# A hybrid attention and SSM layer on one core: a fourth slot in the norm stage, gate products over units 1 to 21, two slots from unit 23, and three smaller edits

## The reference

```python
mod = jax.nn.silu(c) @ w_ada + b_ada            # c: 9 vectors of 2048, w_ada 2048 x 6144
shift, scale, gate = jnp.split(mod, 3, axis=-1)
h = _rmsnorm(x, g_pre) * (1 + scale[:, None]) + shift[:, None]
proj = h @ w_in                                 # q, k, v, z_a, z_b, xbc, dt, r_a, r_b
# A: dilated window attention of three groups (window 128, 512, 2048; dilation 1, 4, 16), 8 heads, times silu(z_a), @ w_o_a
# B: convolution, SSD scan, then
y = y + xs * d_skip[:, None]
yg = y * silu(z_b), in 8 groups of 256 columns
yg = yg * lax.rsqrt(jnp.mean(yg * yg, axis=-1, keepdims=True) + NORM_EPS)
p_b = (yg * g_ssm) @ w_o_b
merged = jax.nn.sigmoid(r_a) * p_a + jax.nn.sigmoid(r_b) * p_b
y_out = x + gate[:, None] * _rmsnorm(merged @ w_o, g_post)
```

## Time and profile before

| | before |
|---|---|
| runs | 3129.91, 3122.58, 3134.31 us |
| profiled execution | 3134.02 us, its span 3132.2 us |
| mean granted PE clock | 0.981 |
| busy: PE, DVE, POOL, ACT | 96%, 65%, 35%, 27% |
| start of unit 1 | 138.91 us |
| start of units 22 and 23 | 454.48 and 467.30 us, 12.8 us for a plain unit |
| a unit with a gate product that waits for nothing | 14.55 us (units 2 to 3: 155.23 to 169.77) |

### The profile page before, as it was taken

The page is one execution under the profiler, slowest core; times in us unless marked ns, Lnnn a source line. Parts: engine busy times, 40 slices in busy tenths (PEclk is TensorE's granted clock), DMA queues, the critical chain, the costliest instruction groups (busy, mean ns, idle before and its releaser), DMA issues. The chain is left out here.

```text
span 3132.2 us, 52927 instructions
## 1 busy us (share of the span) xinstructions
PE 3016.7 (96%) x23068; PEld 2848.9 (91%) x23068; DVE 2036.4 (65%) x2027; ACT 847.8 (27%) x1026; POOL 1099.2 (35%) x368
## 2 busy tenths in 40 slices
PE   5899999999999999999999999999999999999996
PEld 4798999899999999999999999999999989999785
DVE  3301799998994988988888766887777854212202
ACT  2111222232323223233222133333333332212221
POOL 0133233333322333333343343444444423333332
PEclk8899999999999999999999999999999999999998
DMA  8768786654445786646667566666556655766643
GB/s 316 282 245 312 293 300 243 221 201 140 150 134 192 259 292 235 208 180 236 252 238 248 187 228 218 223 217 231 197 196 229 222 193 198 280 248 235 240 170 113
DMA packets 222396, 704.89 MB, mean 225 GB/s; under 512 B 28675, under 2 KB 131835, under 8 KB 172731
## 3 DMA queue, kind: packets, MB, share of 16 engines
q1 hardware_dynamic: 159622, 471.33, 43.9%
q0 software_dynamic: 5248, 174.60, 14.0%
q10 hardware_dynamic: 57296, 55.59, 5.3%
HBM read 630.85 MB, written 245.17 MB: 280 GB/s over the span
## 5 line engine op out<-in xcount | busy, mean ns | idle before, releaser
L1310 PE MATMUL acc<-act,w_hi 128*128 128x288 f32 x5808 | 1742.5, 300 | 18.0 <-POOL w_lo L866 17.9
L1311 PE MATMUL acc<-act,w_hi 128*128 128x288 f32 x5808 | 1715.1, 295 | 0.0
L1312 PE MATMUL acc<-act,w_lo 128*128 128x288 f32 x5808 | 1715.0, 295 | 0.0
L866 POOL TENSOR_TENSOR w_lo<-w_raw,w_hi 128x2048 fp32r<-128x2048 f32 (+1 forms) x209 | 958.0, 4584 | 1986.7 <-ACT w_hi L918 1986.5
L1310 PEld LDWEIGHTS acc<-act,w_hi 128*128 128x128 f32 x5808 | 1092.5, 188 | 43.6 <-issue 20.7
L1311 PEld LDWEIGHTS acc<-act,w_hi 128*128 128x128 f32 x5808 | 1092.7, 188 | 1.8
L1312 PEld LDWEIGHTS acc<-act,w_lo 128*128 128x128 f32 x5808 | 1091.6, 188 | 0.7
L918 ACT ACTIVATE w_hi<-w_raw 128x2048 fp32r<-128x2048 f32 (+1 forms) x209 | 384.7, 1841 | 512.4 <-PE acc L1312 194.4
L1722 DVE TENSOR_TENSOR side<-side 128x2048 f32<-128x2048 f32 x96 | 323.7, 3372 | 70.9 <-DMA side<-in_vals_t 57.8
L1693 DVE TENSOR_TENSOR side<-side 128x2048 f32<-128x2048 f32 x96 | 334.3, 3482 | 51.1 <-DMA side<-in_keys_t 47.2
L984 ACT ACTIVATE ev<-acc 128x576 f32<-128x576 f32 x144 | 93.7, 651 | 787.9 <-PE acc L1312 776.4
(11 more groups left out here) (291 smaller groups left out, 2683.1 us busy)
## 6 DMA issues: line engine op xcount, KB each, us to landing
w_raw<-in_w_in_t SPq DMA_DIRECT2D x160, 1024.0 KB, 7.7
out_s_kv<-in_cache_a_w POOLq DMA_DIRECT2D x80, 1632.0 KB, 9.0
side<-in_keys_t SPq DMA_DIRECT2D x52, 1024.0 KB, 7.3
side<-in_vals_t SPq DMA_DIRECT2D x52, 1024.0 KB, 7.4
w_raw<-in_w_ada_t SPq DMA_DIRECT2D x48, 1024.0 KB, 7.6
out_s_kv<-in_cache_a_w POOLq DMA_DIRECT2D x24, 1344.0 KB, 8.6
w_raw<-in_w_o_b_t SPq DMA_DIRECT2D x16, 1024.0 KB, 7.2
w_raw<-in_w_o_t SPq DMA_DIRECT2D x16, 1024.0 KB, 9.0
```

Of the source, the lines that this page charges most:

```text
L866: nc.gpsimd.tensor_tensor(wl[:, u % 2, 0:kt, 0:cols], raw[:, SLOT[s], 0:kt, 0:cols], wh[:, u % 2, 0:kt, 0:cols].bitcast(F32), ALU.subtract ...
L1310: nc.tensor.matmul(out, wh[:, c, k, 0:cols], high, start=(k == 0), stop=False)
L1311: nc.tensor.matmul(out, wh[:, c, k, 0:cols], low, start=False, stop=False)
L1312: mm = nc.tensor.matmul(out, wl[:, c, k, 0:cols], high, start=False, stop=(k == kt - 1))
```

## The change

The table of slots now has four slots in the norm stage; the fourth lies in a part of `side` that is free there. Gate products are given to the units of `GATE_UNITS`: 1, 2, 3, 5, 6, 7, 9, 10, 12, 13, 14, 16, 17, 18, 20, 21. The units from 23 (`GATES_END + 1`) to `A0 + 3` share two slots, where this began at 111 before. `seen` keeps SP closer to the unit that runs from unit 23 on (6 half units where it was 8), and the store of the gate moves to half unit 48 from 38. `d_skip` comes from an array of 128 x 16 laid out by the host, in one load. In the SSM groups DVE adds the two squares and PE multiplies the sum with the ones. The rectangles of `BAND` are replaced by whole products.

```diff
+GATE_UNITS = [1 + n * 22 // NGATE for n in range(NGATE)]
+GATES_END = GATE_UNITS[-1] + 1
...
-    if 1 <= _u <= NGATE:
-        STREAM.append(("g", _u - 1))
+    if _u in GATE_UNITS:
+        STREAM.append(("g", GATE_UNITS.index(_u)))
...
+PSLOTS = 4
...
-    _few = _kind == "u" and BLOCK0 <= _n < A0 + 4
-    if _few:
-        _slot = _next[1] % 2
-        _next[1] += 1
+    _few = _kind == "u" and GATES_END + 1 <= _n < A0 + 4
+    if _s <= NADA:
+        _slot = _s % PSLOTS
+    elif _few:
+        _slot = (_n + A0) % 2
     else:
+        if _kind == "u" and _n == A0 + 4:
+            _next[0] = 2
         _slot = _next[0] % 3
...
-BAND = ((0, 0, 64), (2, 64, 128), (1, 32, 64), (1, 64, 96), (3, 96, 128))
...
+        fourth = side[:, 15744:15744 + D].rearrange("p (k n) -> p k n", n=P)
+
+        def slot(s):
+
+            return fourth if SLOT[s] == 3 else raw[:, SLOT[s], :, :]
...
-                if s >= 3:
+                if s >= PSLOTS:
                     slot_free(s)
...
+                        else:
+                            sp.wait_ge(gate_out, 16)
...
-                    with nc.allow_non_contiguous_dma(reason="one value a descriptor, once"):
-                        for hh in range(2):
-                            sp.dma_start(dsk[64 * hh:64 * hh + 64, :], A["d_skip"][0:1, hh:SH:2].to_broadcast((64, KT))).then_inc(const_in, 16)
+                    sp.dma_start(dsk, A["d_skip_t"]).then_inc(const_in, 16)
...
-                lag = 8 if u < BLOCK0 else 6 if u < A0 + 2 else 2 if u < A0 + 4 else 4
-                return max(0, 2 * min(u, NGATE + 2) - 4, 2 * u - lag)
+                lag = 8 if u < GATES_END + 1 else 6 if u < A0 + 2 else 2 if u < A0 + 4 else 4
+                return max(0, 2 * min(u, GATES_END + 1) - 4, 2 * u - lag)
...
-                    if half == 2 * NGATE + 6:
+                    if half == 2 * GATES_END + 4:
...
-                    if n == 0:
-                        nc.tensor.matmul(ps_s[:, 0:512], qk[:, 0, r:SEQ:4], qk[:, 3, :], start=True, stop=True)
-                    else:
-                        for x, i0, i1 in BAND:
-                            nc.tensor.matmul(ps_s[i0:i1, x * P:(x + 1) * P], qk[:, 0, 4 * i0 + r:4 * i1:4], qk[:, 3, x * P:(x + 1) * P],
-                                             start=True, stop=True)
+                    nc.tensor.matmul(ps_s[:, 0:512], qk[:, 0, r:SEQ:4], qk[:, 3, :], start=True, stop=True)
...
-                    for x, i0, i1 in BAND:
-                        nc.tensor.matmul(ps_w[i0:i1, P:2 * P], pT[:, x, i0:i1], vP[:, x, :], start=False, stop=False)
+                    for x in range(4):
+                        nc.tensor.matmul(ps_w[:, P:2 * P], pT[:, x, :], vP[:, x, :], start=False, stop=False)
...
-                    pe.wait_ge(ysq_d, g + 1)
+                    pe.wait_ge(ysum, g + 1)
...
-                        for j in range(2):
-                            mm = nc.tensor.matmul(bank[:, 0:HALF], ones[:, :], ysq[:, j, half * HALF:(half + 1) * HALF],
-                                                  start=(j == 0), stop=(j == 1))
+                        mm = nc.tensor.matmul(bank[:, 0:HALF], ones[:, :], ysq[:, 0, half * HALF:(half + 1) * HALF], start=True, stop=True)
...
+                if o == 18:
+                    dve.wait_ge(ysq_d, g + 1)
+                    TT(ysq[:, 0, :], ysq[:, 0, :], ysq[:, 1, :], ALU.add).then_inc(ysum, 1)
```

More of the change, by code:

```diff
@@ L416, in phase_all @@
         c_in, v_in, x_in, const_in = sems("c_in", "v_in", "x_in", "const_in")
-        w_in, ra_in = sems("w_in0", "w_in1", "w_in2"), sems("ra_in0", "ra_in1", "ra_in2")
+        w_in, ra_in = sems("w_in0", "w_in1", "w_in2", "w_in3"), sems("ra_in0", "ra_in1", "ra_in2")
         c_act, c_t, v_t, set_up, pool_set = sems("c_act", "c_t", "v_t", "set_up", "pool_set")
@@ L442, in phase_all @@
         st_t, st_c, p_out = sems("st_t", "st_c", "p_out")
-        yz, ysq_d, ss_t, rt, yr, yn, y_out = sems("yz", "ysq_d", "ss_t", "rt", "yr", "yn", "y_out")
+        yz, ysq_d, ysum, ss_t, rt, yr, yn, y_out = sems("yz", "ysq_d", "ysum", "ss_t", "rt", "yr", "yn", "y_out")
         ma_d, mr_in, mr_d = m.sem("ma_d"), sems("mr_in0", "mr_in1"), m.sem("mr_d")
@@ L518, in _ @@
                     weights(0)
-                if s >= 3:
+                if s >= PSLOTS:
                     slot_free(s)
-                sp.dma_start(raw[:, SLOT[s], :, :].rearrange("p k n -> p (k n)"), A["w_ada_t"][(n % 2) * KT + n // 2]).then_inc(w_in[SLOT[s]], 16)
+                sp.dma_start(slot(s).rearrange("p k n -> p (k n)"), A["w_ada_t"][(n % 2) * KT + n // 2]).then_inc(w_in[SLOT[s]], 16)
             sp.dma_start(causal[:, :], A["causal"]).then_inc(const_in, 16)
@@ L782, in _ @@
                     weights(u)
-                if 1 <= u <= NGATE:
-                    gate_weights(u - 1)
+                if u in GATE_UNITS:
+                    gate_weights(GATE_UNITS.index(u))
                 if u == 1:
@@ L843, in ssm @@
                     if g == 0:
-                        pool.wait_ge(const_in, 176)
+                        pool.wait_ge(const_in, 160)
                     nc.gpsimd.tensor_tensor(Bm, Bt[0:SAMP, 0, :].unsqueeze(1).broadcast_to((SAMP, NB, P)),
@@ L1208, in partial_sums @@
                     q = 32 * (k % 4)
-                    mm = nc.tensor.matmul(ps_s[q:q + 32, (n % 2) * 512:(n % 2) * 512 + P], c32[:, k, :], raw[:, SLOT[src], k, :],
+                    mm = nc.tensor.matmul(ps_s[q:q + 32, (n % 2) * 512:(n % 2) * 512 + P], c32[:, k, :], slot(src)[:, k, :],
                                           start=(k < 4), stop=(k >= KT - 4))
@@ L1571, in _ @@
                 attention(2 * u)
-                if 2 <= u <= NGATE + 1:
-                    gate_rows(u - 2)
+                if u - 1 in GATE_UNITS:
+                    gate_rows(GATE_UNITS.index(u - 1))
                 for g, o in ssm_steps(2 * u):
@@ L1582, in _ @@
                     ssm(g, o)
-                if 1 <= u <= NGATE:
-                    gate(u - 1)
+                if u in GATE_UNITS:
+                    gate(GATE_UNITS.index(u))
                 if u == FOLD0 // 2:
@@ L1854, in dt_part @@
                 if half == 2 * BLOCK0 + 5:
-                    dve.wait_ge(const_in, 176)
+                    dve.wait_ge(const_in, 160)
                     dve.wait_ge(evac, EVACS[u])
@@ L2088, in _ @@
                         low_oa(k)
-                if half % 2 and 1 <= u <= NGATE:
-                    gate_partials(u - 1)
-                if half % 2 == 0 and 2 <= u <= NGATE + 1:
-                    gate(u - 2)
+                if half % 2 and u in GATE_UNITS:
+                    gate_partials(GATE_UNITS.index(u))
+                if half % 2 == 0 and u - 1 in GATE_UNITS:
+                    gate(GATE_UNITS.index(u - 1))
                 for n in grains.get(half - KEYS0, ()):
@@ L2153 @@
          "c_prompt", "c_sample", "b_ada", "g_pre", "g_post", "conv_w", "conv_b", "dt_bias", "a_log",
-         "d_skip", "g_ssm")
+         "g_ssm")
 OUTS = (("y_prompt", (1, SEQ, D)), ("y_sample", (NB, NT, D)),
@@ L2194, in layouts @@
     out["keys_t"], out["vals_t"] = keys, vals
+    out["d_skip_t"] = np.ascontiguousarray(np.repeat(inputs["d_skip"][0].reshape(KT, 2).T, P // 2, axis=0))
     for name in ("w_o_a", "w_o_b"):
```

## The result

The changed kernel took 3100.36 us in the median (3099.99 to 3103.39), the kernel before, run in turn with it, 3130.52: a ratio of 0.9907, interval 0.9892 to 0.9922. That is 30 us, inside the range I gave (3093 to 3128) and on the side I forecast, but the sum of my terms had 18. The profiled execution's span went from 3132.2 to 3098.9 us. The page has PE at 2994.1 us (before 3016.7): 22.6 us less of work and of work at the lower clock together, and some 11 us less waiting.

A forecast was written before the change was run, and what follows sets the result against it. It took TensorE (PE) as the bound, busy 3016.7 of 3132.2 us, so only less PE work or waiting pays. The terms summed to -17.9 us, from the median 3129.9 to 3112 us, range 3093 to 3128.

The forecast's parts named there:

- Norm stage: Before unit 1: a fourth slot shortens waits for w_ada tiles, -10 us; unit 1's weights load later, +0.5.
- rival 1: Norm stage: the DMA queue was full already, so 3 us gained instead of 10; 3119 us, chance 0.17.
- Gate stage: Gate products in units 1 to 21: fewer stalls for POOL, but late DVE copies cancel them; 0 us (-10 to +10).
- Rival 2: Gate stage turns bad: late DVE copies hold PE in units 19 to 22, half clock follows; +10, 3122 us, chance 0.13.
- Two slots: From unit 23: weight loads wait for a later unit, but slack hides it; 0 us.
- d_skip: Near 1790 us: one load in place of two removes PE's wait for POOL and the lost clock; -7.1 us.
- rival 5: The d_skip load was not the cause; small loads around the weight load slow it; 3119 us, chance 0.06.
- SSM groups: Half the ones products -7.8, waits for DVE's addition held by POOL +7.2, work queued behind it +3; net +2.4 us.
- rival 3: Better: POOL does not hold the addition, or the gate stage's stalls go and none come; 3102 us, chance 0.25.
- Attention: Whole products for rectangles: scores -4.4 us, values +0.6 to +8.6 over the steps; net -2 us.
- Output stage: Unit 165 takes the idle third slot, so the 1.74 us wait ahead of unit 166 goes; -1.7 us.
- Rival 4: Slower: the SSM addition blocks DVE's queue; above 3145.6 us from 4.2 us lost a group, 3152 at 5; chance 0.04.

The follow-up runs named there:

- e1: Changed kernel with three slots in the norm stage in place of four; 3111.94 us.
- e4: Changed kernel with the rectangles of BAND back in attention scores and values; 3105.54 us.
- e7: Changed kernel with the SSM groups' product with the ones 12 matmuls later, for groups that end before the output stage; 3099.82 us.
- e2: Changed kernel with the gate products back in units 1 to 16; 3103.0 us.
- e8: Changed kernel with each gate row product, and DVE's addition to it, one unit later; 3085.71 us.
- e6: Changed kernel with three slots in units 23 to 110, two only from 111; 3103.89 us.
- e11: e8 with three slots in units 23 to 110; 3088.11 us, beside 3085.71 for e8.
- e3: Changed kernel with d_skip loaded by two strided loads again; 3106.45 us.
- e12: Changed kernel with gate row products one unit later, ones product 12 matmuls later, and the old slot table from unit 1; 3081.47 us.
- e5: Changed kernel with four products with the ones again and no addition on DVE in the SSM groups; 3101.69 us.

## Why the prediction was right, and where it was off

The time was in the range and the sign was right; the size was short by 12 us in the medians (15 in the profiles). Some 5 us of the profile's gain, at the attention step, is luck, as said below. By its steps:

- **Norm stage**, -9.5 with unit 1's load, came out -11.5 (e1: 12). That three slots bound the stage was right, and rival 1, a full queue, is out. But the working was half right. I took 365 GB/s for what the queue gives when it is never short of requests, and it went to 406 to 419; the trace of the kernel before has 395 from 20 to 30 us already. And I expected the wait for tiles to fall to about 15 us, and it fell from 25.9 to 20.2 only. About half of the gain is the clock, a term that my sum did not have here (an estimate from the two rows of the kernel before: 9.87 x 0.32 + 7.98 x 0.34 = 5.9 us). The figure of 358 GB/s for the memory side (the Trainium skill, "DMA: Bandwidth & Descriptors", section "Where 436 GB/s comes from") was passed by these rows, so it bounds nothing here.
- **Gate stage**, 0: from unit 1 to unit 32 it came out -0.7. The parts had the signs that I argued and were larger: -9.6 to unit 11, +13.7 from there to 23, and then -4.8 at the attention step, which I had not in the sum and which is luck: e4 and e7, the same program up to there, wait there as long as the kernel before. Over the five profiles of that program the stage comes out between -3.0 and +8.2, and e2 agrees with a net near zero. Rival 2 had the mechanism, waits for late copies with the lower clock behind them, and not the net. The place was half right: I had the copies late in units 19 to 22, and a wait of 4.15 us is there (unit 19), but the longest, 4.84, is in unit 11. What I did not see is that this wait was avoidable at no cost (e8).
- **Two slots**, 0: right from unit 40 on (e6, e11); ahead of it the runs do not tell.
- **d_skip**, -7.1: -8.4 in this pair of traces, 4.7 in e3. The mechanism is shown, and rival 5 is out. The size depends on the execution: the kernel before had a second wait there (1.2 us for ACT at 1838.49) that I had not counted, e3 has only the first, 1.8 us long, and less time at the lower clock.
- **SSM groups**, +2.4: +0.3 for the seven groups up to unit 161, and some -1.0 for the eighth. The chain to the ones product was as worked out: the addition held to the end of POOL's subtraction, and six waits, of 0.92 us and not 1.2. The +3 for what stands behind the addition came to nothing: two of those operations take 1.88 and 2.13 us beside POOL's next ones, where they took 0.42 and 0.41 before, but PE does not wait for them. The Trainium skill ("SBUF — State Buffer", section "Who interferes with whom") has this lock between DVE with two inputs in SBUF and GpSimd, and the trace agrees: 4.00 us beside POOL, 0.75 when begun ahead of it. The first half of rival 3, an addition that is not held, is out, and e7 shows how its gain is to be had.
- **Attention**, -2: -4.4. The term for the values was mis-sized: 12 records take 1.27 us (600.19 to 601.46) and not 1.32 to 1.57, where the banded step took 1.30, so the two parts do not cancel. e4 gives 4.6.
- **Output stage**, -1.7: -6.0 from unit 165 to 177, and this is the term that was most off. I counted one wait of 1.74 us. A second one, of 1.3 us before the state product, hung on the same slot, and e12 gives 3.4 for both. The last group's norm saved 1.0. The remaining 1.6 is the clock: PE ran at a mean of 0.83 from 2610 to 2620 us, behind the second wait, and at 1.00 in the same units after the change. With the old slots e12 has both waits and a clock of 1.00 behind them, so this last part may belong to the one execution of the kernel before.

```profile
2610.00:2620.00 10.00, 8.66 (x48) 7.70 (x47) 6.87 (x12) 1.24 (x3) 2.38 (x1) 0.83 0.40 143
```

```profile
2581.00:2591.00 10.00, 10.00 (x70) 9.07 (x70) 8.32 (x14) 2.51 (x4) 4.80 (x2) 1.00 0.80 282
```

(The first is of the kernel before, the second of the changed one.) Unit 161 went the other way, +1.5, unit 177 gave -1.6, and the stretch behind unit 178 gave -2.5. The table of lengths above shows that units 161 and 177 move by as much between executions, and behind unit 178 the profiles of kernels that are the same program there lie between 424.6 and 430.9 us (428.5 before, 426.0 after). So of the 8.7 us that the pair of traces gains behind unit 161, some 4.4 are shown to be lasting; the medians gained 30.2 where the profiles gained 33.3.

Rival 4 (PE losing more than 4 us a group) had no sign in the trace: PE's next products did not wait.

## What to carry to other kernels

A wait that the main engine makes for a small result of a busy engine is often a matter of where the consumer stands in the program: one row product a unit later gave 15 us, and one 12 matmuls later took six waits away. Where the trace shows that an operation is held to the end of another engine's instruction, as DVE's addition is here (4.00 us for 0.75), leave room for that whole instruction between producer and consumer. Split a large change by the starts of its units, since a net of zero in one stage (here -10 and +14) hides the gain that can still be had. And before a difference in one stretch is put down to an edit, compare that stretch in the profiles of runs that are the same program there: unit 177 alone moves by 2 us.

## What was not expected of the hardware

- The DMA queues moved 419 GB/s from 100 to 110 us (share 1.01) on loads of 1 MB, once four slots took them; with three the same stretch had 286, and 304 in e1.
- A wait of 2.6 us for a tile had 20 us at a mean clock of 0.68 and 0.66 behind it (kernel before), and about half of what the norm stage gained is this.
- Two loads with 4-byte pieces held the next 1 MB load for 31.1 us (29.7 in e3), with a longest landing of 12.5 without them.
- The same program came to unit 23 up to 8.5 us earlier or later from one execution to the next. The waits for DVE's copy fall in other units and lengths each time (4.84, 0.28, 0.88, 4.15 and 1.17 us in the changed kernel; 5.31, 4.83, 2.15, 1.71 and 0.97 in e5); what sets them was not traced further. A change in such a stage needs either many runs or a reading of the trace stretch by stretch.
